# Attention heads in pairs, spare weight buffers, a router on the unnormalised residual, and rounded token-major expert traffic in a two-block fp32 model

## The reference, cut to what matters

```python
mod = (c_act @ w_mod[l] + b_mod[l])[:, None, :]
shift_m, scale_m, gate_m, shift_f, scale_f, gate_f = jnp.split(mod, 6, axis=-1)
h = rms_norm(x, norm_mix[l]) * (1.0 + scale_m) + shift_m
...   # z = h @ w_in; o_a (8 heads, window 128), o_b (RG-LRU), o_c (8 heads, causal)
merged = g[:, :, 0] * p_a + g[:, :, 1] * p_b + g[:, :, 2] * p_c
x = x + gate_m * (merged @ w_out[l])
h = rms_norm(x, norm_ffn[l]) * (1.0 + scale_f) + shift_f
u = causal_dwconv(h @ w_up[l], ffn_conv_w[l], ffn_conv_b[l])
x = x + gate_f * ((jax.nn.silu(u_gate) * u_val) @ w_down[l])
```

```python
logits = (xt @ w_router).astype(jnp.float32)          # xt = rmsnorm(h, norm_ffn_g[1])
top_vals, top_idx = lax.top_k(logits, TOP_K)
top_w = jax.nn.softmax(top_vals, axis=-1)
...
for e in range(N_EXPERTS):                            # D_EXPERT = 3584
    y = y + combine[:, e:e + 1] * swiglu(xt, w_gate[e], w_up[e], w_down[e])
return rmsnorm(h, norm_final_g)
```

## Time and profile before

| | |
|---|---|
| time, median of 3 runs | 2370.84 us (2370.57 to 2370.88) |
| time of the profiled execution | 2369.96 us |
| its span, first to last instruction | 2368.2 us |
| mean granted TensorE clock | 0.973 |
| busy: PE, DVE, ACT | 2232.5, 1749.6, 1328.3 us |
| DMA from HBM | 562.37 MB, 238 GB/s over the span |
| chain of waits, share by engine | PE 80%, DVE 9%, ACT 4% |

### The profile page before, as it was taken

One profiled execution on the slowest core, in us unless ns is written; L12 is line 12 of the kernel. 1 busy time (PEld: TensorE's weight loads), 2 busy tenths in 40 slices (PEclk: granted clock), 3 DMA queues, 4 the chain that ended last, 5 costly groups with the idle time before them and its releaser, 6 DMA issues.

```text
span 2368.2 us, 35018 instructions
## 1 busy us (share of the span) xinstructions
PE 2232.5 (94%) x13975; PEld 1997.1 (84%) x13975; DVE 1749.6 (74%) x1928; ACT 1328.3 (56%) x1288; POOL 75.8 (3%) x159
## 2 busy tenths in 40 slices
PE   6999998999989899999897799999999999999997
PEld 4988987999978899999787688888888888888886
DVE  5668855884795555558864588888888888888885
ACT  3564433653534444345343576777676777777674
POOL 5011200000000000000000000000000000000000
PEclk9999999999999999999899799999999999999998
DMA  9637746756544356555342499989999999989992
GB/s 274 181 122 228 238 156 167 197 175 187 160 134 143 90 144 188 172 177 164 114 163 82 159 374 338 372 321 371 336 367 347 347 374 335 369 318 374 333 368 110
DMA packets 415499, 566.51 MB, mean 239 GB/s; under 512 B 17098, under 2 KB 268212, under 8 KB 415344
## 3 DMA queue, kind: packets, MB, share of 16 engines
q1 hardware_dynamic: 410160, 556.31, 68.8%
q0 software_dynamic: 4896, 6.89, 1.2%
q10 hardware_dynamic: 288, 1.05, 0.1%
HBM read 562.37 MB, written 1.84 MB: 238 GB/s over the span
## 4 chain that ended last, share of the span: by engine, by line
PE 80%; DVE 9%; ACT 4%; issue 2%; DMA 0%; ACTq 0%; SPq 0%; DVEq 0%
PE pair L1045 58%; PE misc L1045 13%; DVE wlo L1578 2%; DVE arena L1926 2%; PE misc L1451 1%; PE pair L1462 1%; PE misc L1486 1%; ACT whi L612 1%; PE misc L1115 1%; PE misc L1230 1%; PE misc L1099 0%; PE misc L1363 0%; DVE rt L1603 0%; DMA raw<-in_w_up_dram 0%; PE misc L1271 0%
## 5 line engine op out<-in xcount | busy, mean ns | idle before, releaser
L2122 DVE TENSOR_TENSOR wlo<-raw,whi 128x2048 fp32r<-128x2048 f32 x338 | 769.8, 2289 | 124.4 <-ACT whi L976 123.4
L976 ACT CAST whi<-raw 128x2048 fp32r<-128x2048 f32 x338 | 646.9, 1917 | 202.8 <-PE misc L1045 101.2
L1045 PE MATMUL pair<-hh,whi 128*128 128x256 f32 x1840 | 532.4, 289 | 24.0 <-DVE hl L1596 19.6
L1578 DVE TENSOR_TENSOR wlo<-raw,whi 128x2048 fp32r<-128x2048 f32 (+1 forms) x174 | 385.1, 2215 | 210.6 <-ACT whi L612 209.9
L1045 PE MATMUL pair<-hl,whi 128*128 128x256 f32 x1840 | 526.5, 286 | 0.0
L1045 PE MATMUL pair<-hh,wlo 128*128 128x256 f32 x1840 | 526.2, 286 | 0.0
L1045 PE MATMUL pair<-whi,oph 128*128 128x512 f32 (+1 forms) x1024 | 394.4, 385 | 4.8 <-DVE wlo L2122 3.1
L1045 PE MATMUL pair<-wlo,oph 128*128 128x512 f32 (+1 forms) x1024 | 386.6, 378 | 0.0
L1045 PE MATMUL pair<-whi,opl 128*128 128x512 f32 (+1 forms) x1024 | 385.9, 377 | 0.0
L1045 PEld LDWEIGHTS pair<-hh,whi 128*128 128x128 f32 x1840 | 359.3, 195 | 30.9 <-issue 26.4
L612 ACT CAST whi<-raw 128x2048 fp32r<-128x2048 f32 (+1 forms) x174 | 320.6, 1843 | 87.4 <-PE pair L1045 72.9
(11 more groups left out here) (418 smaller groups left out, 2502.1 us busy)
## 6 DMA issues: line engine op xcount, KB each, us to landing
raw<-in_moe_w_gate_dram SPq DMA_DIRECT2D x114, 1024.0 KB, 7.0
raw<-in_moe_w_up_dram SPq DMA_DIRECT2D x112, 1024.0 KB, 7.0
raw<-in_moe_w_down_dram SPq DMA_DIRECT2D x112, 1024.0 KB, 6.8
raw<-in_w_in_dram SPq DMA_DIRECT2D x38, 1024.0 KB, 5.3
raw<-in_w_mod_dram SPq DMA_DIRECT2D x24, 1024.0 KB, 5.9
raw<-in_w_up_dram SPq DMA_DIRECT2D x44, 512.0 KB, 5.2
raw<-in_w_xkv_dram SPq DMA_DIRECT2D x16, 1024.0 KB, 5.5
raw<-in_ffn_w_gate_dram SPq DMA_DIRECT2D x22, 512.0 KB, 3.9
```

The costliest lines, as they stand in the source:

```text
L976: act.copy(whi[:, q, :], raw[:, r, :]).then_inc(sem("hi_ready"), 1)
L1045: ins = pe.matmul(out_, lhs, rhs, start=start and i == 0, stop=stop and i == 2)
L1578: dve.tensor_tensor(wlo[:, i_ % SPLIT, 0:size], raw[:, raw_of(n), 0:size], whi[:, i_ % SPLIT, 0:size].bitcast(F32), ALU.subtract).then_inc ...
L2122: dve.tensor_tensor(wlo[:, q, :], raw[:, r, :], whi[:, q, :].bitcast(F32), ALU.subtract).then_inc(sem("lo_ready"), 1)
```

## The change

In `plan` the 22nd modulator slot moves behind `w_out` and the 24th behind the second group of `up`; the last three go to the two buffers of `raw` that the ring doesn't use, and each load waits for whatever was last in its own buffer (the first two of these three for the end of the merge). Scores are issued for two heads at once, alternating between the lower and the upper 64 rows, and so are the outputs. The router's scalings by the gain go to ACT, chunk pair by chunk pair beside the groups of `xo`; logits are made from the unnormalised residual, and the root of the mean square per token (`token_root`, `token_rs`) is applied to the difference of the two best and where the tokens are split. The gather is for two experts at once, in two rounded parts, five times rather than nine; the scatter is token-major into `x_acc`, rounded, a quarter at a time at j = 1, 2, 5 and 6 of the next expert, and the weight of a token is applied when `ye` is split. The last norm is token-major.

```diff
+SPARE_MODS = {0: RING, 1: RING + 1, 21: RING, 22: RING + 1, 23: RING}
+LATE_SPARE = (21, 22)
+SCATTER_AT = (1, 2, 5, 6)
...
     for j in range(4):
         dense("w_out", w["w_out"][0], [(j * 256, 256)], "dve")
-        modulator(j == 0)
     modulator(2)
     for j in range(FC):
         dense("up", w["w_up"][0], [(j * P, P), (FF + j * P, P)], "dve")
+        modulator(j == 1)
...
+            if plain_no.get(n) in SPARE_MODS:
+                raw_at[n] = SPARE_MODS[plain_no[n]]
+            else:
+                raw_at[n] = ring_no % RING
+                ring_no += 1
...
-                    if n >= RAW:
-                        j = plain_no.get(n - RING)
+                    if plain_no.get(n) in LATE_SPARE:
+                        sp.wait_ge(sem("merged_f"), 4)
+                    elif freed_by[n] is not None:
+                        j = plain_no.get(freed_by[n])
...
             def scores(h):
...
                 if h >= 2:
-                    pe.wait_ge(sem("att_max"), 2 * (h - 1))
+                    pe.wait_ge(sem("att_max"), 2 * h)
                 for i, (qb, kb) in enumerate(((0, 0), (1, 0), (1, 1))):
+                    for b in range(2):
+                        q, k, _ = operands(h + b)
+                        ins = pe.matmul(misc[:, b, i * P:(i + 1) * P], q[:, qb * P:(qb + 1) * P], k[:, kb * P:(kb + 1) * P],
+                                        start=True, stop=True)
...
+            def outputs(h):
+                o = att_bank(h // 2)
+                for kb, cols, pt in ((0, slice(0, T), slice(0, T)), (1, slice(P, T), slice(T, 384))):
+                    for b in range(2):
+                        _, _, v = operands(h + b)
+                        ins = pe.matmul(o[64 * b:64 * b + 64, cols], v[:, kb], pt_buf[b][:, pt], start=(kb == 0), stop=(kb == 1))
...
             for j, g in enumerate(stage_groups["w_out"]):
                 add_modulated(g, j, 16)
-                if j == 0:
+                if j == 1:
                     mod_slot(21)
...
+            def routed(j):
+                pe.wait_ge(sem("h_scaled"), DC * NORM["ffn1"] + 2 * j + 2)
+                for c in (2 * j, 2 * j + 1):
+                    for i in range(TB):
+                        ins = pe.matmul(misc[:, 2 + i, 0:NE], work[:, c, i * P:(i + 1) * P], rw[:, c, :],
+                                        start=(c == 0), stop=(c == DC - 1))
...
+                pe.wait_ge(sem("sq_ready"), 4 * NORM["ffn1"] + j + 1)
+                for c in (2 * j, 2 * j + 1):
+                    for i in range(TB):
+                        ins = pe.matmul(misc[:, i, 0:1], router_sq[:, c, i * P:(i + 1) * P], ones[:, 0:1],
+                                        start=(c == 0), stop=(c == DC - 1))
...
+            def gather(G):
+                pe.wait_ge(sem("m_gt"), G + 1)
+                for b in range(4):
+                    for c in range(2):
+                        f = (2 * b + c) * P
+                        for k, part in enumerate((hn_hi, hn_lo)):
+                            for i in range(TB):
+                                ins = pe.matmul(banks[:, b, c * T:(c + 1) * T], part[:, i, f:f + P],
+                                                place[:, i].rearrange("p u s -> p (u s)"), start=(k == 0 and i == 0), stop=(k == 1 and i == 1))
...
+            def scatter(r, dst, cb, E):
...
+                pe.matmul(dst, comb_t[cb][:, tok], ye_hi[:, cols], start=True, stop=False)
+                pe.matmul(dst, comb_t[cb][:, tok], ye_lo[:, cols], start=False, stop=True).then_inc(sem("m_s"), 1)
...
                     gate_or_up(j, 0)
                     if j >= 1:
                         turn(j - 1)
+                    if j in SCATTER_AT:
+                        r = SCATTER_AT.index(j)
+                        pe.wait_ge(sem("m_added"), S * 4 + (r + 4))
...
+                        scatter(r, misc[:, 1, :], 1 - u, E + 1)
                     gate_or_up(j, 1)
-                    if j >= 1:
+                    if j == JE - 1:
+                        down(j - 1, (0,))
+                        turn(j)
+                        down(j - 1, (1,))
+                    elif j >= 1:
                         down(j - 1)
...
-                gather(Q + 1)
-                turn(JE - 1)
-                scatter(Q, 1 - u, E + 1)
+                if u == 1:
+                    gather(G + 1)
                 down(JE - 1)
...
+                act.activation(ye_hi, misc[:, 2:4, :].rearrange("p a b -> p (a b)"), ACT.Copy, scale=weigh_slot[:])\
...
+                dve.scalar_tensor_tensor(ye_lo, misc[:, 2:4, :].rearrange("p a b -> p (a b)"), weigh_slot[:], ye_hi.bitcast(F32),
+                                         ALU.mult, ALU.subtract).then_inc(sem("m_yl"), 1)
...
+            dve.tensor_tensor_reduce(work[:, 4:8, :].rearrange("p a b -> p (a b)"), x_acc[:, 1], x_acc[:, 1], 1.0, 0.0, ALU.mult, ALU.add,
+                                     tiny[:, 6, 1:2]).then_inc(sem("fin_sq"), 1)
...
+            for q in range(4):
+                i, cols = q // 2, slice((q % 2) * 512, (q % 2 + 1) * 512)
+                dve.scalar_tensor_tensor(x_acc[:, i, cols], x_acc[:, i, cols], token_rs[:, i:i + 1], final_gain[:, cols], ALU.mult, ALU.mult)\
```

More of the change, by code:

```diff
@@ L1237, in _ @@
             scores(0)
-            scores(1)
             spread_roots(range(6, 10))
@@ L1262, in _ @@
                     mod_columns(7 + h)
[L1263 to L1272 removed]
+                if h % 2:
+                    if h >= 2:
+                        pe.wait_ge(sem("att_out_lo"), h // 2)
+                    if h in (1, 9):
+                        pe.wait_ge(sem("act_read"), reads_at[stage_groups["va"][0] if h == 1 else stage_groups["vc"][1]])
+                    outputs(h - 1)
             mod_product(20)
@@ L1441, in _ @@
             pe.matmul(misc[:, 0, 16:16 + NE], ones[:], sel[:, 1], start=False, stop=True).then_inc(sem("ranked"), 1)
-            pe.wait_ge(sem("hn_tok"), 4)
-            def gather(Q):
-                pe.wait_ge(sem("m_gt"), Q + 1)
-                for half in range(2):
-                    for c in range(4):
-                        f = (4 * half + c) * P
-                        for i in range(TB):
-                            ins = pe.matmul(misc[:, 1 - half, c * P:(c + 1) * P], hn_tok[:, i, f:f + P], place[:, i, :],
-                                            start=(i == 0), stop=(i == 1))
+            pe.wait_ge(sem("x_copied"), 4 + 2)
@@ L1453, in gather @@
                     ins.then_inc(sem("m_x"), 1)
-            def scatter(S, cb, E):
+            def scatter(r, dst, cb, E):
                 pe.wait_ge(sem("m_yc"), E)
+                pe.wait_ge(sem("m_yl"), E)
                 pe.wait_ge(sem("m_c"), E)
-                for r in range(4):
-                    for m in range(2):
-                        f = (2 * r + m) * P
-                        ins = pe.matmul(banks[:, r, m * T:(m + 1) * T], ye[:, f:f + P], comb_t[:, cb], start=True, stop=True)
-                    ins.then_inc(sem("m_s"), 1)
@@ L1471, in gate_or_up @@
                         q = (n_split + k) % SPLIT
+                        if j == 0 and kind == 0:
+                            pe.wait_ge(sem("m_xlo"), G * 4 + (2 * half + 2))
                         pe.wait_ge(sem("lo_ready"), E * MOE_SLOTS + (n_split + k + 1))
@@ L1843, in _ @@
                 ahead_of(beside[h], 1 if h < 12 else 2)
-                if h % 2 == 0 and h >= 2:
-                    out_low(h // 2 - 1)
-                if h < 12:
-                    mod_slot(8 + h)
+                if h % 2 == 0:
+                    if h >= 2:
+                        out_low(h // 2 - 1)
+                    normalised(h + 1)
+                    if h < 12:
+                        mod_slot(8 + h)
+                    if h + 2 < NHEAD:
+                        peak(h + 2)
+                else:
+                    if h + 2 < NHEAD:
+                        peak(h + 2)
+                        normalised(h + 1)
+                    if h < 12:
+                        mod_slot(8 + h)
             branches(3)
```

336 lines of the change are left out of this document (185 added, 151 removed).

## The result

The changed kernel took 2308.45 us (median of 4 executions, 2306.62 to 2311.53), the one before 2370.7 on the same chip: a ratio of 0.9747, 95% interval 0.9734 to 0.9759. Forecast were 2305.0, range 2291 to 2323. The profiled execution took 2310.16 us with a span of 2308.0, 60.2 less than before.

| stretch | before | after | difference | forecast |
|---|---|---|---|---|
| start to the first scores | 173.3 | 172.0 | -1.4 | 0 |
| first scores to `mod_product(20)` (attention) | 160.4 | 147.0 | -13.3 | -10 |
| to the first `up` group (merge, `w_out`, norm) | 65.6 | 56.1 | -9.5 | -10.5 |
| to the second head's output in the last cross-attention (not touched) | 861.8 | 869.3 | +7.5 | 0 |
| to the first expert product (the other two heads and `xo`, router, gather) | 73.6 | 55.1 | -18.5 | -16 |

What follows compares the result with a forecast made beforehand. TensorE was taken to bound the experts, with idle waits at w_out, router and tail; savings 10 + 10.5 + 16 + 19.2 + 10.1 = 65.8 us gave a 2302.4 span, plus 1.8 and 0.9, 2305.1 us, range 2291 to 2323.

Steps and rivals of the forecast that it cites:

- the likeliest case: Whole kernel: the forecast of 2305.1 us holds, own range 2294 to 2314, chance 0.73.
- Attention: Heads: pairing scores and outputs of two heads saves 10 us, bounds 3 (no overlap) and 13 (full overlap).
- Rival (b): Heads: paired passes do not overlap, 7 us less gained (only 3 saved), 2312 us; chance 0.08.
- VectorE's lead: Heads: VectorE falls behind by 0.3 us a head, but its 4 us lead over TensorE lasts the twelve heads.
- The step w_out: w_out and the norm behind it: earlier modulator slots and w_up loads save 10.5 us, bounds 6 and 11.
- Router: Last xo to first expert product: earlier logits and shorter preparation save 16 us, bounds 10 and 19.
- the bound: Router's lower bound: gather's 32 passes at half clock again (6.48 us), ScalarE's copies fully on the path; only 10 us saved.
- Experts: Four expert pairs: less TensorE work saves 4.8 us a pair, 19.2 in all; bounds 0 and 24.
- the stop of 1.1 at the loop's edge stays: Edge between expert pairs: the 1.1 us stop stays, set by ScalarE's rounding and the splitting behind it as before.
- Tail: After the last expert: quartered scatter and token-major norm take 18.2 us for 28.3, saving 10.1; bounds 8 and 12.
- (a): Experts: loads hold the pace at 250.9 us a pair, only 2 of 19 us gained, 2322 us; chance 0.15.
- (c): Experts: quartered scatter stops TensorE at 32 places, 2.29 us each, +73.3, 2378 us; chance 0.04.

Runs made afterwards that it cites:

- changed_again: The changed kernel run once more, unchanged, with a profile of its own; median 2306.71 us, ratio 0.9731 to the kernel before.
- The held loads: Changed kernel with SP's load of slot 4 of experts 2, 4 and 6 waiting until TensorE used the previous expert's last slot; 2300.16 us, one execution.
- slot40_first: Changed kernel with VectorE splitting slot 40 ahead of the last hidden_lo instead of behind it; 2311.93 us, ratio 0.9758 to the kernel before.
- pe_loop_unrolled: Changed kernel with TensorE's loop over pairs of experts written out four times, other engines keeping their loops; 2310.57 us.
- heads_in_turn: Changed kernel with the paired heads' scores and outputs issued one head behind the other instead of alternating; 2310.05 us.
- middle_shifted: Changed kernel with the 16 products of mod_product(22) made four times over, delaying everything from up on; medians 2318.24 us, then 2320.37 us.

## Why the prediction was right, and where it was not

**The sum.** 2308.45 for 2305.0, inside the likeliest case's own range; the terms gave 65.8 and the stretches 60.2. The one large difference, +7.5, is in a stretch that the change doesn't touch: TensorE was granted 1.2 GHz there in places where it had 2.4 before. A second profile of the same kernel had 3.6 less. One profile of before was my base, and it happened to hold the shortest length seen for this stretch. That the sum came so near is in part luck: start, attention and router gave 7.2 us more than forecast, and `w_out`, experts and tail 5.3 less.

**Attention, -13.3 for -10.** Right in kind, wrong in size and partly in the reason. I priced overlap by the passes. What a round shows is closer to a price of each stay in the small tiling: the second head's outputs behind the first cost 0.01 to 0.02, alternating or not, and its scores 0.01 alternating, 0.33 in turn. Scores were 0.87 for my 0.97, outputs 0.80 for 1.02, and I had left out the 0.29 of neighbours that are delayed once instead of twice. The 13.3 also holds some clock: in changed_again, where the second round had a higher one, the stretch took 145.6 us, 14.7 less than before. Rival (b) fell in its number: even without alternation 11 us are saved, not 3.

**VectorE's lead.** The prediction said that it "lasts the twelve heads". It did, and the stops behind them, at the merge, are those of the kernel before. The step w_out, -9.5 for -10.5, is 11.0 at equal clock; in the changed kernel's profile half clock took 1.5 back, which the prediction didn't foresee. The sum of squares was 1.13 for 0.87, the products 7.00 for 7.1.

**Router, -18.5 for -16.** The three pairs of logits beside `xo` cost 1.68 each, 0.8 above the sums they replace, as priced. The gain over the forecast lies in equal parts ahead of the `pick` row, 35.6 us behind the start of the last head's output for 36.7, and behind it, 11.8 us to the first expert product for 13. The gather did run at half clock for most of its 6.76 us, as the bound had it, but it starts the experts as soon as its quarters are split.

**Experts, -15.6 for -19.2.** Two terms were mis-sized. The body of a pair, without the stop at its edge, is 246.0 to 246.3 us, for 245.7 forecast (246.8 less the stop of 1.1): the scatter's 16 products took 4.38 (0.55 for two; I had 0.46), the weights' column 0.9 more for 0.7, and 13.68 was taken away, not 14.06; gather 3.83 for 3.97 and the new stop 0.85 for 0.9 were right. And the step "the stop of 1.1 at the loop's edge stays" failed. That stop, for the splitting of the third slot, was covered by another one ahead of the first slot, of 2.22, 1.68 and 1.31, and the loads that used to be idle at that moment now run without a pause. The held loads and the written-out loop show from both sides that the new stop needs both, TensorE's jump and full DMA engines; in either run it is gone and the old one is back in its place, 1.08 and 1.32.

**Tail, -9.4 for -10.1.** 18.9 us for 18.2. The quarters were scattered at half clock, 0.43 us a product, so that the additions ended 7.2 us in and not 6.1; the last DMA then took 2.5 for 3.0.

**Rivals (a) and (c).** The loads reach 393 GB/s. TensorE never waited at a place of the scatter.

## What to carry to other kernels

The gain of work taken off a saturated engine is found where predicted, but what used to wait at the same time moves too: a shorter pair filled the DMA queues at the loop's edge, and the jump back, free before, cost up to 2.2 us, in some profiles followed by half clock. Remove such stops together (loop written out, splitting reordered), since slot40_first and pe_loop_unrolled alone gave nothing here that the time shows. And don't take a single profile's length of a stretch with idle gaps as exact to more than 1%: here the same instructions took 861.8 to 871.0 us by the clock granted.

## What the runs showed that was not expected

- Twelve fp32 passes of 64 rows for two heads on the two halves of the array, alternating, last 0.87 us, as six for one head; in turn 1.19. Eight passes on two column halves last 0.80 alternating and 0.81 in turn, for 0.79 of four.
- A jump back in TensorE's loop costs nothing with idle DMA engines, 1.3 to 3.0 us with full ones (a wait that the profile puts down to VectorE's splitting at some edges and to "issue" at others; at 2043.00 the splitting named elsewhere wasn't even over).
- Stops of 2.28, 2.99 and 2.33 us in the middle of dense work were followed by some 3.5 us at half clock, stops of 2.22, 1.68 and 1.31 were not; a stop of 1.83 in changed_again was. The length of the stop doesn't decide it: at the edges of heads_in_turn 1.92 and 1.85 were followed by half clock and 2.54 was not, in middle_shifted 1.82 and 1.93 were and 2.46 was not.
- A conditional jump over a long, untaken branch left VectorE idle for 3.1 to 3.4 us, for 0.36 with the work ahead of it; ScalarE's table load at the head of a loop body went with the loop.
- The loads held 392 to 393 GB/s for two pairs of experts.
